# Start offsets of the moving rows of 512-column products, and one VectorE addition moved, in a chained three-block kernel

## What is computed

```python
# first block, for layer in range(2)
h = h + mix
h = h + squared_relu_mlp(rmsnorm(h, mlp_norm[layer]), w_mlp_up[layer], w_mlp_down[layer])
...
# second block
y_mix, q_mem = gdn_branch(u @ gdn_w_in[j], ...)
f = swiglu(rms_norm(h, norm_pre_ffn[layer]), w_ffn_in[layer], w_ffn_out[layer])
h = h + rms_norm(f, norm_post_ffn[layer])
```

## Time and profile before

| | us |
|---|---|
| median of 3 runs | 1866.86 (1864.90 to 1867.52) |
| the profiled execution | 1861.33 |
| its span, first to last instruction | 1859.5 |
| PE busy | 1816.1 (98%) |
| VectorE (DVE) busy | 1313.9 (71%) |
| ScalarE (ACT) busy | 929.4 (50%) |
| mean granted TensorE clock | 0.996 of full |

### The profile page before, as it was taken

How to read it: one execution, slowest core, us unless ns; L and a number is a source line. 1 busy time by engine, 2 the same in 40 slices (tenths; PEclk the granted TensorE clock), 3 DMA queues, 4 the chain that set the end, 5 groups by cost and what they waited for, 6 DMA issues and landing times.

```text
span 1859.5 us, 31153 instructions
## 1 busy us (share of the span) xinstructions
PE 1816.1 (98%) x12498; PEld 1661.0 (89%) x12498; DVE 1313.9 (71%) x1890; ACT 929.4 (50%) x1566; POOL 33.1 (2%) x31
## 2 busy tenths in 40 slices
PE   7999999999999999999999999999999999999997
PEld 7888878999999999898889878887889898999996
DVE  4664476767777775877777768878738379877775
ACT  5456444544344446654334433645667464544553
POOL 0100001200000000000000000000000000000000
PEclk9999999999999999999999999999999999999998
DMA  5211101232223232332323322222201422333331
GB/s 198 71 57 58 60 1 46 80 98 95 92 91 112 82 119 80 114 102 92 102 91 114 102 91 94 86 70 80 80 1 34 138 81 90 114 103 102 109 108 57
DMA packets 63364, 162.55 MB, mean 87 GB/s; under 512 B 4632, under 2 KB 29464, under 8 KB 63096
## 3 DMA queue, kind: packets, MB, share of 16 engines
q1 hardware_dynamic: 62368, 158.59, 25.8%
q10 hardware_dynamic: 856, 2.00, 0.3%
HBM read 156.38 MB, written 4.19 MB: 86 GB/s over the span
## 4 chain that ended last, share of the span: by engine, by line
PE 85%; DVE 7%; ACT 3%; DMA 1%; DVEq 1%; issue 1%; ACTq 0%; SPq 0%
PE ps L725 73%; PE ps L1408 2%; DMA USLF<-W 1%; PE ps L948 1%; DVE wlo L3409 1%; PE ps L1277 1%; DVE wlo L3039 1%; PE ps L1413 0%; PE ps L1256 0%; PE ps L1254 0%; PE ps L923 0%; PE ps L1352 0%; ACT WU L2647 0%; PE ps L924 0%; PE ps L1548 0%
## 5 line engine op out<-in xcount | busy, mean ns | idle before, releaser
L725 PE MATMUL ps<-UH,whi 128*128 128x264 f32 (+1 forms) x696 | 203.0, 292 | 9.3 <-DVE wlo L3039 9.3
L725 PE MATMUL ps<-USH,whi 128*128 128x512 f32 (+1 forms) x584 | 207.3, 355 | 0.8 <-DVE USL L3962 0.7
L725 PE MATMUL ps<-USL,whi 128*128 128x512 f32 (+1 forms) x584 | 202.4, 347 | 0.0
L725 PE MATMUL ps<-UL,whi 128*128 128x264 f32 (+1 forms) x696 | 198.3, 285 | 0.0
L725 PE MATMUL ps<-UH,wlo 128*128 128x264 f32 (+1 forms) x696 | 197.9, 284 | 0.0
L1976 ACT ACTIVATE whi<-raw 128x1024 fp32r<-128x1024 f32 x114 | 119.3, 1052 | 82.7 <-PE ps L725 63.1
L725 PE MATMUL ps<-KFH,whi 128*128 128x264 f32 x512 | 145.8, 285 | 1.6 <-DVE KFL L3451 1.5
L725 PE MATMUL ps<-KFH,wlo 128*128 128x264 f32 x512 | 145.3, 284 | 0.0
L725 PE MATMUL ps<-KFL,whi 128*128 128x264 f32 x512 | 145.2, 284 | 0.0
L725 PEld LDWEIGHTS ps<-UH,whi 128*128 128x128 f32 (+1 forms) x696 | 131.1, 188 | 10.5 <-issue 9.5
L725 PE MATMUL ps<-TH,whi 128*128 128x256 f32 x504 | 139.1, 276 | 0.0
(11 more groups left out here) (596 smaller groups left out, 5094.0 us busy)
## 6 DMA issues: line engine op xcount, KB each, us to landing
raw<-W SPq DMA_DIRECT2D x134, 512.0 KB, 3.5
raw_p<-W SPq DMA_DIRECT2D x46, 1024.0 KB, 5.0
ULF<-W SPq DMA_DIRECT2D x22, 512.0 KB, 3.9
USLF<-W SPq DMA_DIRECT2D x22, 512.0 KB, 4.0
raw_d<-W SPq DMA_DIRECT2D x14, 512.0 KB, 3.7
H<-xT SPq DMA_DIRECT2D x4, 528.0 KB, 6.8
spill<-H SPq DMA_DIRECT2D x1, 2048.0 KB, 7.1
H<-spill SPq DMA_DIRECT2D x1, 2048.0 KB, 8.8
```

Of the source, the lines that this page charges most:

```text
L725: mm = pe.matmul(dst, a, b, start=start and n == 0, stop=stop_ and n == 2, skip_group_check=again)
```

## The change

1. The hidden rows of MLP1 and of ffn are split in two buffers: rows 0 and 1 of each four start at 128 modulo 256, rows 2 and 3 at 192. Row lists (`four_rows`) replace the slices `[:, f % 4, :]`.
2. The inputs of `gin` and of ffn's plain tiles lie in new tiles `GUH`/`GUL` at `u_at`, 128 modulo 256. MLP1's own inputs stay in `USH`/`USL` at 192.
3. `MTH`, `MTL` and `FOM` move by 256 bytes and stay at 192; `TH` and `TL` don't move.
4. In MLP1's pairs with two pieces VectorE does `piece_out(after[0], 0)` ahead of `after_lo(i, 1)`. MLP0 keeps its order.

Numbers of instructions, matmuls, DMAs and semaphore increments stay the same.

```diff
+ROW = SEQ * 4
+ENDROWS = 2
...
-        TH, TL, FH0, FL0, FH1, FL1, GA0, GA1 = region(
-            S0, ("TH", [P, 7, 4, NMEM], FR), ("TL", [P, 7, 4, NMEM], FR), ("FH0", [P, 4, SEQ], FR), ("FL0", [P, 4, SEQ], FR),
-            ("FH1", [P, 4, SEQ], FR), ("FL1", [P, 4, SEQ], FR), ("GA0", [P, SEQ], F32), ("GA1", [P, SEQ], F32))
+        TH, TL = region(S0, ("TH", [P, 7, 4, NMEM], FR), ("TL", [P, 7, 4, NMEM], FR))
+        f_end = S0 + 2 * 7 * 4 * NMEM * 4
+        f_at = f_end + 4 * ENDROWS * ROW + 192
+        FE = region(f_end, *[(n, [P, ENDROWS, SEQ], FR) for n in ("FEH0", "FEL0", "FEH1", "FEL1")])
+        FB = region(f_at, *[(n, [P, 4 - ENDROWS, SEQ], FR) for n in ("FBH1", "FBL1", "FBH0", "FBL0")])
...
+        def four_rows(begin, end):
+            return [begin[:, k, :] for k in range(4 - ENDROWS)] + [end[:, k, :] for k in range(ENDROWS)]
+        FH0, FL0, FH1, FL1 = (four_rows(b, e) for b, e in zip(FB, FE))
...
+        m_at = S0 + 3 * ENDROWS * ROW + 192
+        ME = region(S0, *[(n, [P, ENDROWS, SEQ], FR) for n in ("MEH0", "MEL0", "MEH1")])
+        MB = region(m_at, *[(n, [P, 4 - ENDROWS, SEQ], FR) for n in ("MBH0", "MBL0", "MBH1")])
+        MFH0, MFL0, MFH1 = (four_rows(b, e) for b, e in zip(MB, ME))
...
-        t_at = S0 + 3 * 8192 + 2048
+        t_at = S0 + 3 * 8192 + 2048 + 256
...
+        GUH, GUL = region(u_at, ("GUH", [P, KT, SEQ], FR), ("GUL", [P, KT, SEQ], FR))
...
             def us(k):
-                return USH[:, k, :]
+                return GUH[:, k, :]
...
                     if some == 2:
                         hidden_lo(f)
                         hidden_lo(f + 1)
+                        if p.layer:
+                            piece_out(after[0], 0)
                         after_lo(i, 1)
-                        piece_out(after[0], 0)
+                        if not p.layer:
+                            piece_out(after[0], 0)
                         after_lo(i, 2)
```

More of the change, by code:

```diff
@@ L429, in build @@
         b11, b21, t2, t1, t3, b22, t4 = range(7)
-        MFH0, MFL0, MFH1, GM0 = region(
-            S0, ("MFH0", [P, 4, SEQ], FR), ("MFL0", [P, 4, SEQ], FR), ("MFH1", [P, 4, SEQ], FR), ("GM0", [P, SEQ], F32))
-        GM1, = region(masks_at, ("GM1", [P, SEQ], F32))
-        t_at = S0 + 3 * 8192 + 2048
-        MTH, MTL, FOM, MFL1 = region(
-            t_at, ("MTH", [P, 4, 4, NMEM], FR), ("MTL", [P, 4, 4, NMEM], FR), ("FOM", [P, KT, SEQ], F32), ("MFL1", [P, 4, SEQ], FR))
-        assert t_at + 16384 >= S0 + 20480 + 8960 + 32 and t_at + 32768 + 16384 + 8192 <= AB0
+        m_at = S0 + 3 * ENDROWS * ROW + 192
+        ME = region(S0, *[(n, [P, ENDROWS, SEQ], FR) for n in ("MEH0", "MEL0", "MEH1")])
+        MB = region(m_at, *[(n, [P, 4 - ENDROWS, SEQ], FR) for n in ("MBH0", "MBL0", "MBH1")])
+        MFH0, MFL0, MFH1 = (four_rows(b, e) for b, e in zip(MB, ME))
+        GM0, = region(m_at + 3 * (4 - ENDROWS) * ROW, ("GM0", [P, SEQ], F32))
+        GM1, = region(masks_at, ("GM1", [P, SEQ], F32))
+        t_at = S0 + 3 * 8192 + 2048 + 256
+        MTH, MTL, FOM, MEL1 = region(
+            t_at, ("MTH", [P, 4, 4, NMEM], FR), ("MTL", [P, 4, 4, NMEM], FR), ("FOM", [P, KT, SEQ], F32), ("MEL1", [P, ENDROWS, SEQ], FR))
+        MBL1, = region(t_at + 32768 + 16384 + ENDROWS * ROW + 192, ("MBL1", [P, 4 - ENDROWS, SEQ], FR))
+        MFL1 = four_rows(MBL1, MEL1)
+        assert t_at + 16384 >= S0 + 20480 + 8960 + 32 and t_at + 32768 + 16384 + 8192 + 192 <= AB0
         XT, = region(t_at + 16384, ("XT", [P, 4, 4, NMEM], F32))
-        total_m, = region(S0 + 16384, ("total_m", [P, L], F32))
+        total_m, = region(m_at + 2 * (4 - ENDROWS) * ROW, ("total_m", [P, L], F32))
         KFH0, KFL0, KFH1, KFO = region(
@@ L447, in build, with each_row @@
         KFL1, = region(END - 4 * L * 4, ("KFL1", [P, 4, L], FR))
+        def each_row(x):
+            return [x[:, k, :] for k in range(4)]
         KG_0, KG_1 = region(gates_at, ("KG_0", [P, L], F32), ("KG_1", [P, L], F32))
@@ L455, in build @@
         m1, m3, m4, m2 = range(4)
-        space0 = Space(L, HALF, [KFH0, KFH1], [KFL0, KFL1], [KG_0, KG_1], KTH, KTL, KX, KFO, UF[:, 0:4, HALF:L],
+        space0 = Space(L, HALF, [each_row(KFH0), each_row(KFH1)], [each_row(KFL0), each_row(KFL1)], [KG_0, KG_1], KTH, KTL, KX, KFO, UF[:, 0:4, HALF:L],
                        ULF[:, 0:4, HALF:HALF + 2 * P], UH, UL, R2[:, :], R[1][:, :], ((7, 5, 6), (4, 5, 6)))
@@ L463, in fh @@
         def fh(f):
-            return (FH0, FH1)[f // 4 % 2][:, f % 4, :]
+            return (FH0, FH1)[f // 4 % 2][f % 4]
         def fl(f):
-            return (FL0, FL1)[f // 4 % 2][:, f % 4, :]
+            return (FL0, FL1)[f // 4 % 2][f % 4]
         ps = ctx.enter_context(nc.psum_tensor("ps", [P, 8, 512], F32))
@@ L776, in us @@
             def us(k):
-                return USH[:, k, :]
+                return GUH[:, k, :]
             def usl(k):
-                return USL[:, k, :]
+                return GUL[:, k, :]
             def memory_sum():
@@ L789, in hidden @@
                 def hidden(f):
-                    return h.high[f // 4 % 2][:, f % 4, :]
+                    return h.high[f // 4 % 2][f % 4]
                 def hidden_rest(f):
-                    return h.low[f // 4 % 2][:, f % 4, :]
+                    return h.low[f // 4 % 2][f % 4]
                 def block_passes(t, v, at, f, start, stop):
@@ L1959, in hi @@
                 if m >= 3:
-                    act.activation(USH[:, k, :], H[:, k, META:L], ACT.Copy, scale=g).then_inc(uh_done, 1)
+                    act.activation((USH if m == 3 else GUH)[:, k, :], H[:, k, META:L], ACT.Copy, scale=g).then_inc(uh_done, 1)
                 else:
@@ L2353, in hidden_hi @@
                     act.wait_ge(relu2_done, base + f + 1)
-                    act.activation(h.high[f // 4 % 2][:, f % 4, :], h.gates[f % 2][:, :], ACT.Copy).then_inc(hh_done, 1)
+                    act.activation(h.high[f // 4 % 2][f % 4], h.gates[f % 2][:, :], ACT.Copy).then_inc(hh_done, 1)
                 def mlp_plain(j):
@@ L2848, in input_hi @@
                     v = VEC["pre_ffn"] + k
-                    act.activation(USH[:, k, half(x)], H[:, k, part(x)], ACT.Copy, scale=vecs[:, v:v + 1]).then_inc(uh_done, 1)
+                    act.activation(GUH[:, k, half(x)], H[:, k, part(x)], ACT.Copy, scale=vecs[:, v:v + 1]).then_inc(uh_done, 1)
             def input_squares(x):
@@ L3007, in lo @@
                 if m >= 3:
-                    dve.scalar_tensor_tensor(USL[:, k, :], H[:, k, META:L], g, USH[:, k, :].bitcast(F32), ALU.mult,
+                    high, low = (USH, USL) if m == 3 else (GUH, GUL)
+                    dve.scalar_tensor_tensor(low[:, k, :], H[:, k, META:L], g, high[:, k, :].bitcast(F32), ALU.mult,
                                              ALU.subtract).then_inc(u_done, 1)
@@ L3450, in hidden_lo @@
                     dve.wait_ge(hh_done, base + f + 1)
-                    dve.tensor_tensor(h.low[f // 4 % 2][:, f % 4, :], h.gates[f % 2][:, :], h.high[f // 4 % 2][:, f % 4, :].bitcast(F32), ALU.subtract).then_inc(hid_done, 1)
+                    dve.tensor_tensor(h.low[f // 4 % 2][f % 4], h.gates[f % 2][:, :], h.high[f // 4 % 2][f % 4].bitcast(F32), ALU.subtract).then_inc(hid_done, 1)
                 def scale_squared():
@@ L3961, in input_lo @@
                     dve.wait_ge(uh_done, 40 + 8 * x + k + 1)
-                    dve.scalar_tensor_tensor(USL[:, k, half(x)], H[:, k, part(x)], vecs[:, v:v + 1],
-                                             USH[:, k, half(x)].bitcast(F32), ALU.mult, ALU.subtract).then_inc(u_done, 1)
+                    dve.scalar_tensor_tensor(GUL[:, k, half(x)], H[:, k, part(x)], vecs[:, v:v + 1],
+                                             GUH[:, k, half(x)].bitcast(F32), ALU.mult, ALU.subtract).then_inc(u_done, 1)
             def input_sum(x):
```

4 lines of the change are left out of this document (3 added, 1 removed).

## The result

The changed kernel takes 1868.5 us (median of 20 runs, 1865.8 to 1871.8), the kernel before in the same session 1864.4 us (20 runs, 1856.7 to 1867.8). The ratio is 1.0022, with a 95% interval from 1.0014 to 1.0031: slower, by 4 us or 0.2%, where I forecast 1858.6 (8.3 us faster, a ratio of 0.9956). The profiled execution took 1865.87 us, 4.5 more than the profiled one of before.

What follows compares the result with a forecast made beforehand. TensorE, busy for 98% of the span, was taken to bound the kernel. Terms of -2.3, -2.2, +0.1 and -3.9 us summed to -8.3, from a median of 1866.86 to 1858.6 us, with a range from 1856 to 1870.5.

Steps and rivals of the forecast that it cites:

- The lock of the pairs: All pairs of 256-column products in MLP1 and ffn take the quick pace; 11 of MLP1's pairs gain: -3.9 us.
- case A: All pairs of MLP1 and ffn are quick: 1858.6 us; chance 0.40.
- case D: All pairs of MLP1 and ffn are slow: 1869.9 us; chance 0.13.
- "As today's tiles end on", and "whose pieces run without holes": Reasons for quick pairs: six products at 192 end like today's tiles, and ffn, without holes, is quick every time.
- Hidden rows: In MLP1 and ffn, 648 products at 128 gain 1.5 us, offset changes in about 100 tiles cost 1.6: +0.1 us.
- gin and plain tiles: 984 products of 512 columns in gin, its gates and ffn's plain tiles reach the 226.7 ns floor: -2.2 us.
- The 256-column halves: ffn's 192 halves and 48 of the last hidden rows, at 117.5 ns, could gain 1.0 us; put at 0.
- The addition: In MLP1's pairs with two pieces, adding ahead of the low part removes TensorE's waits: -2.3 us.
- Case B: Offsets do nothing anywhere, only the moved addition gains: 1864.6 us; chance 0.20.
- Case E: Rows at 128, level with the weights, collide; every product there takes 233.5 ns: 1871.9 us; chance 0.12.
- case C: Offsets help, but the pairs stay mixed in pace: 1862.5 us; chance 0.15.

Runs made afterwards that it cites:

- the addition alone: The kernel before with only VectorE's addition moved ahead of the low part in MLP1's pairs: 1861.9 against 1860.9 us, ratio 1.0007.
- the slow profile of before: The kernel before, unchanged, profiled once more: 1867.66 us.
- the hidden rows alone: The kernel before with only the split of the hidden rows between 128 and 192: 1869.7 against 1860.9 us, ratio 1.0053.

## Why the prediction was wrong

*The lock of the pairs* is the step that failed: "I take the quick one: six products are two rounds of the cycle of three". The mechanism was as put: the last 512-column product decides, all pairs of a kernel with the split have one pace, and ffn goes with MLP1. But the six don't run two rounds. Behind the change to 192 come three products out of the cycle (234, 236, 229), then a long, a short and a middle one (231, 226, 229), so that the sixth is the middle one. With four in place of six behind the change all 32 pairs are quick, and the ratio, 0.9965, is near the 0.9956 that case A would have been. This is case D, priced at 1869.9: +7.4 for the pairs, and 21 pairs x 0.37 = +7.8 by the profiles. The warning was in the earlier trace rows, where the first products after a change of offset were 16 ns longer: I priced those 16 ns and left out that they also shift the place.

*"As today's tiles end on", and "whose pieces run without holes".* This was the second fault. ffn's first pieces have a hole of 1.4 us in the trace before too, behind the product at 1552.88. ffn of before is quick in one profile and slow in the next, and I took its 18 of 18 as the rule, where it was one draw carried on 18 times. It also fits that the medians are only 4 us apart and the two profiles, without their first stretch, 6.8: the runs of before hold both kinds (1855.4 to 1868.9 in the study), those of the change only the slow one (1865.8 to 1871.8). The 20 runs of before in that session have no clock on record, so for them this is argued.

*Hidden rows*: +0.1 forecast. The products go from 229.0 to 231.3 ns, and between two kernels whose MLP1 pairs are all slow the stretch goes from 259.64 (the addition alone) to 260.73. ffn's goes from 234.97 (before, slow) to 235.81. With +0.35 in MLP1's last tiles and +0.24 in ffn's (58.28 against 58.04 in the slow profile of before) that is about +2.5. It was mis-sized by its missing half: I counted 16 ns once per tile and nothing for the way back. 2.3 ns x 12 = 28 ns a tile is what both cost together. The gain at 128 never comes: in this order the six there have distances of 234, 231, 233, 236, 224, 230.

*gin and plain tiles*: -2.2 forecast, the floor of 226.7 ns was right (distances of 226, 227, 227 in gin and in ffn's plain tiles), but gin gave -1.06 us, since about ten products of each entry are off it. The 24 gate products gained nothing (6.45 us in both traces). The 256-column halves, which I put at 0, go from 117.7 to 120 ns: the +0.40 of the table.

*The addition*: -2.3 forecast, by the way put forward: it runs in the idle time ahead of the low part, and no wait took its place. Alone it is worth 2.9 us of MLP1's stretch against the first profile of before, and (261.43 - 259.64) + 0.37 = 2.2 against the second; between the hidden rows alone and the whole change, both all slow, 261.80 - 260.73 = 1.1, as the holes differ from one execution to the next.

*The rivals.* Case B is refuted: with `ENDROWS` alone at 0, 4 or 2, which changes nothing but addresses, a piece's products take 227.5, 229.0 or 231.3 ns and the kernel 1864.7, 1855.0 or 1868.5 us. The Trainium skill's page "TensorE: Matmul & The Clock Gate" (Part 2, "Step-by-step: what each phase is for") has loading weights and moving data on two independent read ports, and has the load take nothing from the running matmul. How many ports there are no run here shows; the second half doesn't agree with the earlier trace rows, where the moving rows stay at 192, the weights' offset changes and 226.7 ns become 233.5. The same section gives 215.7 ns for 512 columns back to back; here, with a load for each product and in this 32-bit format, it is 226.7 at best in any steady stretch. Case E (233.5 at 128) didn't come, as gin's 226.7 in a steady stretch shows; case C's mixed pairs are what the kernel before has.

## What to carry to other kernels

In a kernel that TensorE bounds, look at the distances of starts to the nanosecond before you believe in a pace: a lock can be handed on for hundreds of microseconds from one product, so a figure that "18 of 18" show may be one draw. Take a second profile of the unchanged kernel before you rest a forecast on such a figure, and look at the granted clock of each stretch before you compare two of them. An address change is then priced by the place at which each stretch ends, not by its mean pace. And a version that makes the place certain is worth more than one that gains 2 ns a product: nothing but the order of twelve products took the change from 1.0022 to 0.9965 of the time of before, with a spread of 4.5 us over its runs in place of 13.

## What was not expected of the hardware

- 256-column products at one and the same pair of offsets have two steady paces, 113.3 and 117.8 ns, and all 18 of ffn's (84 products each) take the one or the other together. With one product of 0.23 us put into the tile ahead, the place passed from long to short and all 18 were slow in that profile.
- With the weights at 128 modulo 256, the pace of 512 columns is 226.7 ns with the moving rows at 128, 229 with them at 192, and 231 to 232 where they alternate between the two in each tile; 256 columns at 128 are worse off than at 192, 120 ns. Whether the rows' offset counts by itself or by its distance from the weights' was not tried on these products.
- A disturbance of 20 ns over five products, without any wait, moved the place. What it is, and what decides the place behind ffn's hole, stays open.
- By the paces, quickest of all would be rows at 128 (227.5 ns) with quick pairs; that is not shown. No order tried gives both, since pairs entered from the steady 227 are slow.
